# Head norms by an inverse root with one Newton step, and head sums of layer 0 in two rounded passes

## The reference

```python
def _rms_norm(x, g):
    xf = x.astype(jnp.float32)
    y = xf * lax.rsqrt(jnp.mean(xf * xf, axis=-1, keepdims=True) + EPS) * g.astype(jnp.float32)
    return y.astype(x.dtype)
...
            q = _rope(_rms_norm(q, p["q_norm_att"][j]), pos)
            k = _rope(_rms_norm(k, p["k_norm_att"][j]), pos)
...
        qx = _rms_norm(qx.reshape(n, t, N_X_HEADS, HEAD_DIM), p["q_norm_x"][i])
```

## Time and profile before

| | us |
|---|---|
| median of 3 runs (lowest, highest) | 1167.59 (1166.1, 1168.38) |
| the profiled execution | 1164.45 |
| its span, first to last instruction | 1162.7 |
| PE busy in the span | 1137.8 (98%) |
| DVE busy | 804.2 (69%) |
| ACT busy | 522.2 (45%) |
| POOL busy | 130.7 (11%) |

### The profile page before, as it was taken

How to read it: one execution, slowest core, us unless ns; L and a number is a source line. 1 busy time by engine, 2 the same in 40 slices (tenths; PEclk the granted TensorE clock), 3 DMA queues, 4 the chain that set the end, 5 groups by cost and what they waited for, 6 DMA issues and landing times.

```text
span 1162.7 us, 22189 instructions
## 1 busy us (share of the span) xinstructions
PE 1137.8 (98%) x8998; PEld 1098.3 (94%) x8998; DVE 804.2 (69%) x1201; ACT 522.2 (45%) x902; POOL 130.7 (11%) x140
## 2 busy tenths in 40 slices
PE   5999999999999999999999999999999999999998
PEld 5899646999999999999999999999999999999998
DVE  6789975798577468558658545689856846756853
ACT  7623786366136227326433232446713722732630
POOL 0038752000000000000240131200000000000000
PEclk9999999999999999999999999999999999999999
DMA  8543141223313213312622321131331332231231
GB/s 336 189 160 119 51 166 52 73 74 109 109 37 122 103 67 108 108 64 81 216 73 73 146 87 64 71 110 61 122 108 39 111 108 72 96 121 44 101 137 48
DMA packets 23146, 120.18 MB, mean 103 GB/s; under 512 B 2708, under 2 KB 6932, under 8 KB 9892
## 3 DMA queue, kind: packets, MB, share of 16 engines
q1 hardware_dynamic: 17892, 100.93, 24.7%
q0 software_dynamic: 1632, 10.54, 2.5%
q10 hardware_dynamic: 3552, 7.74, 1.9%
HBM read 111.29 MB, written 5.69 MB: 101 GB/s over the span
## 4 chain that ended last, share of the span: by engine, by line
PE 94%; DVE 2%; ACT 2%; POOL 1%; DMA 0%; issue 0%; ACTq 0%; DVEq 0%; POOLq 0%
PE zps L505 53%; PE zps L779 25%; PE ops L779 4%; PE zps L767 4%; PE tps L649 1%; PE ops L677 1%; PE tps L534 1%; POOL sm L1900 1%; DVE w_lo L929 1%; PE zps L603 1%; ACT w_hi L1410 1%; ACT act_hi L1410 1%; DVE sm L1063 0%; PE zps L610 0%; PE tps L610 0%; DMA memx<-memT 0%
## 5 line engine op out<-in xcount | busy, mean ns | idle before, releaser
L505 PE MATMUL zps<-act_hi,w_hi 128*128 128x272 f32 x1664 | 348.6, 291 | 0.9 <-DVE w_lo L929 0.9
L505 PE MATMUL zps<-act_hi,w_lo 128*128 128x272 f32 x1664 | 344.0, 288 | 0.0
L505 PE MATMUL zps<-act_lo,w_hi 128*128 128x272 f32 x1664 | 343.2, 288 | 0.0
L779 PE MATMUL zps<-xf,wf 128*128 128x272 f32 x2304 | 298.7, 289 | 0.1
L779 PEld LDWEIGHTS zps<-xf,wf 128*128 128x128 f32 x2304 | 294.1, 188 | 0.7 <-issue 0.3
L505 PEld LDWEIGHTS zps<-act_hi,w_hi 128*128 128x128 f32 x1664 | 262.2, 188 | 5.4 <-issue 2.9
L505 PEld LDWEIGHTS zps<-act_lo,w_hi 128*128 128x128 f32 x1664 | 261.5, 188 | 0.0
L505 PEld LDWEIGHTS zps<-act_hi,w_lo 128*128 128x128 f32 x1664 | 260.0, 189 | 0.0
L1410 ACT ACTIVATE w_hi<-w_stage 128x2048 fp32r<-128x2048 f32 (+1 forms) x61 | 114.7, 1883 | 151.3 <-PE zps L505 123.9
L929 DVE TENSOR_TENSOR w_lo<-w_stage,w_hi 128x2048 fp32r<-128x2048 f32 x59 | 137.6, 2333 | 43.5 <-ACT w_hi L1410 43.2
L1410 ACT ACTIVATE wf<-w_sum 128x1024 fp32r<-128x1024 f32 x64 | 67.9, 1061 | 195.4 <-DVE w_sum L947 90.4
(11 more groups left out here) (184 smaller groups left out, 1270.4 us busy)
## 6 DMA issues: line engine op xcount, KB each, us to landing
w_stage<-wst SPq DMA_DIRECT2D x92, 1024.0 KB, 4.9
kx<-xkT POOLq DMA_DIRECT2D x4, 1024.0 KB, 8.6
vx<-xv POOLq DMA_DIRECT2D x4, 1024.0 KB, 7.0
x_res<-xT ACTq DMA_DIRECT2D x2, 1088.0 KB, 7.8
tmp<-z ACTq DMA_DIRECT2D x32, 68.0 KB, 2.1
yT<-x_res ACTq DMA_DIRECT2D x7, 272.0 KB, 2.1
memx<-memT SPq DMA_DIRECT2D x2, 512.0 KB, 4.6
vb<-swav POOLq DMA_DIRECT2D x1, 1024.0 KB, 9.9
```

Source lines behind the costliest of these rows:

```text
L505: mm = pe.matmul(zps[slot][:, h, 0:n], w_[:, d, k, w:w + 128], r_[:, k, c0 + h * n:c0 + (h + 1) * n], start=(j == 0 and i == 0), stop=(j = ...
L779: mm = pe.matmul(bank, wf_hl[pw][:, fw, a, :], x_form(l, px, fx, a)[:, 0, :], start=(begin and a == 0 and j == 0), stop=(a == KC // 2 - 1 ...
```

## The change

In `root_heads` ScalarE takes Abs_reciprocal_sqrt in place of Sqrt (result y0), then squares y0 in a second instruction. VectorE, in place of the reciprocal, makes one Newton step in two SCALAR_TENSOR_TENSOR: (sum + 64 eps) y0^2, which reads `tps` again, then that minus 192, times y0; the factor -1/128 is folded into the gain (`hgain_n`, made once). The product with the gain stays. `tps` is now free for the next head sum when VectorE's first instruction is through (`n_dev`), where it was when the Sqrt was (`n_sd`).

For the ten panels of layer 0, ScalarE also rounds the squares to fp32r (`sq_hi`), VectorE forms the rest (`sq_lo`, in `square_lo`, ahead of `head_norm`), and the head sum is two fp32r products per half with a rounded block of ones (`head_r`). The two tiles lie in memory that is free in this stage. The two norms of layer 1 keep the float32 head sum.

```diff
@@ headsum
+                if n < N_QX[1]:
+                    pe.wait_ge(h_rdy, 1)
+                    pe.wait_ge(n_lo, n + 1)
+                    take(tfree)
+                    for h in range(2):
+                        c = slice(h * HALF, (h + 1) * HALF)
+                        pe.matmul(tps[:, h, 0:HALF], head_r[:, :], sq_hi[:, n % 2, c], start=True, stop=False)
+                        mm = pe.matmul(tps[:, h, 0:HALF], head_r[:, :], sq_lo[:, n % 2, c], start=False, stop=True)
+                    mm.then_inc(n_ms, 1)
+                    tfree[0] = (n_dev, n + 1)
+                    return
                 pe.wait_ge(n_sq, n + 1)
...
-                tfree[0] = (n_sd, n + 1)
+                tfree[0] = (n_dev, n + 1)
@@ head_norm
-                dve.wait_ge(n_sd, n + 1)
+                dve.wait_ge(n_inv2, n + 1)
                 taken(dve, *norm_panel(n))
-                link(dve.reciprocal(tmp[:, 3, :], tmp[:, 2, :]))
+                y0, y0_sq = tmp[:, 2, :], tmp[:, 3, :]
+                dve.scalar_tensor_tensor(out=halves(y0_sq), in0=tps[:, :, 0:HALF], scalar=HD * EPS, in1=halves(y0_sq),
+                                         op0=ALU.add, op1=ALU.mult).then_inc(n_dev, 1)
+                dve.wait_ge(n_dev, n + 1)
+                link(dve.scalar_tensor_tensor(out=y0_sq, in0=y0_sq, scalar=-3.0 * HD, in1=y0, op0=ALU.add, op1=ALU.mult))
...
+            def square_lo(n):
+                dve.wait_ge(n_hi, n + 1)
+                dve.tensor_tensor(sq_lo[:, n % 2, :], tmp[:, n % 2, :], sq_hi[:, n % 2, :].bitcast(f32), ALU.subtract).then_inc(n_lo, 1)
@@ DVE, start
+            link(dve.tensor_scalar(hgain_n[:, :], con[:, C_HG:C_HG + 4], -0.5 / HD, None, ALU.mult))
@@ DVE, loop of 12 rounds
+                if i < 10:
+                    square_lo(i)
                 if 1 <= i <= 10:
                     head_norm(i - 1)
@@ ACT, root_heads
-                root(src, dst, HD, n_ms, n + 1, n_sd, (n_out, n + 1))
+                act.wait_ge(n_ms, n + 1)
+                act.wait_ge(*sd_free[0])
+                act.activation(halves(tmp[:, 2, :]), tps[:, :, 0:HALF], ACT.Abs_reciprocal_sqrt, bias=eps, scale=1.0 / HD).then_inc(n_inv, 1)
+                act.wait_ge(n_inv, n + 1)
+                act.activation(tmp[:, 3, :], tmp[:, 2, :], ACT.Square).then_inc(n_inv2, 1)
+                sd_free[0] = (n_out, n + 1)
@@ ACT, square
                 act.activation(tmp[:, n % 2, :], norm_src(n), ACT.Square).then_inc(n_sq, 1)
+                if n < N_QX[1]:
+                    act.wait_ge(n_sq, n + 1)
+                    copy(sq_hi[:, n % 2, :], tmp[:, n % 2, :]).then_inc(n_hi, 1)
@@ ACT, start
+            copy(head_r[:, :], headones).then_inc(h_rdy, 1)
```

More of the change, by code:

```diff
@@ L92, in build_kernel @@
     sm1, _ = place("sm1", [128, 6, 260], at=at_act[1] + 12 * NT * 4)
+    sq_hi, _ = place("sq_hi", [128, 2, NT], f32r, at=at_act[1] + 12 * NT * 4)
+    sq_lo, _ = place("sq_lo", [128, 2, NT], f32r, at=at_act[1] + 14 * NT * 4)
     z1, _ = place("z1", [128, 2, NT], at=at_act[0])
@@ L122, in build_kernel @@
     con, _ = place("con", [128, C_N])
+    head_r, _ = place("head_r", [128, 128], f32r)
+    hgain_n, _ = place("hgain_n", [128, 4])
     nsink, _ = place("nsink", [128, 16])
@@ L169, in build_kernel @@
         s_full, s_sd, s_rstd = sem("s_full"), sem("s_sd"), sem("s_rstd")
-        n_sq, n_ms, n_sd, n_out = (sem("n_" + s) for s in ("sq", "ms", "sd", "out"))
+        n_sq, n_ms, n_inv, n_inv2, n_dev, n_out = (sem("n_" + s) for s in ("sq", "ms", "inv", "inv2", "dev", "out"))
+        h_rdy, n_hi, n_lo = sem("h_rdy"), sem("n_hi"), sem("n_lo")
         r_sw, r_out = [sem(f"r_sw{i}") for i in range(2)], sem("r_out")
@@ L996, in head_norm_out @@
                 src = norm_src(n)
-                dve.scalar_tensor_tensor(out=src, in0=src, scalar=hgain(norm_gain(n)), in1=tmp[:, 3, :],
+                dve.scalar_tensor_tensor(out=src, in0=src, scalar=hgain_n[:, norm_gain(n):norm_gain(n) + 1], in1=tmp[:, 3, :],
                                          op0=ALU.mult, op1=ALU.mult).then_inc(n_out, 1)
+            def square_lo(n):
+                dve.wait_ge(n_hi, n + 1)
+                dve.tensor_tensor(sq_lo[:, n % 2, :], tmp[:, n % 2, :], sq_hi[:, n % 2, :].bitcast(f32), ALU.subtract).then_inc(n_lo, 1)
             def key_sums(m):
@@ L1434, in root_heads @@
             def root_heads(n):
-                src, dst = tps[:, :, 0:HALF], halves(tmp[:, 2, :])
-                root(src, dst, HD, n_ms, n + 1, n_sd, (n_out, n + 1))
+                act.wait_ge(n_ms, n + 1)
[4 more added lines that the diff above has]
+                sd_free[0] = (n_out, n + 1)
             def square(n):
```

## The result

The changed kernel takes 1170.79 us in the median of 6 runs (1170.09 to 1171.74), the kernel before 1166.18 (6 runs, 1164.29 to 1168.38): a ratio of 1.0036, 95% interval [1.0023, 1.0049], some 4.2 us slower. 1170.9 had been forecast. The profiled execution took 1170.19 us.

The account below looks back on a forecast made before the run. PE was taken to bound the kernel, 94% of the chain. Early rounds -0.5 us, six later rounds +3.2 to +4.6, the rest 0: +3.3 taken, on the median of 1167.59 giving 1170.9 us; range 1165.0 to 1173.5.

Parts of the forecast that it names:

- Head sums: On PE in layer 0: ten head sums fall from 0.92 to 0.50 us each, 4.2 us saved if PE never waits.
- The first head sum: Rounding and rest of squares come before it, so PE starts 1.0 to 1.4 us late; 1.2 us lost.
- The table load: One more ScalarE load of 1.28 us in round 1, lying under panel 2; cost 0.
- Inverse root 0.70 and first Newton step 0.78: Durations in us assumed for ScalarE's inverse root and VectorE's first Newton step, the latter needing no port.
- rival C: Worse: first Newton step takes the port too, or release of `tps` holds the head sum; +6 to +7 us; 0.08 with D.
- The port: VectorE instructions with two SBUF inputs and GpSimd's exclude each other; demand rises from 5.97 to 7.47 us per round.
- The size of the rounds: Six rounds from 4 to 10 take 7.47 to 7.7 us in place of 6.93: +3.2 to +4.6 us.
- GpSimd's last product: The last rotary product in the stage ends 3 to 6 us later, at 127 to 131 us.
- Attention and layer 1: Attention moves as a whole, and PE does not wait for layer 1's norms; 0 us each.
- A: Rival, not slower: the port does not bind, PE gets 4.2 us less 1.2; -3.0 us, 1164.6; chance 0.20.
- B: Rival, same: one new user takes the port or both fall into GpSimd's idle time; -1 to +1.5 us, 1167.8; chance 0.20.

Follow-up runs that it names:

- a_norope: The changed kernel with GpSimd's rotary products cut to 32 of 544 columns; ratio 0.9961 to the kernel before, stage 74.15 us.
- s_only: The changed kernel with only the two rounded head-sum passes, root and reciprocal kept from the kernel before; ratio 1.0078 to the kernel before, stage 84.67 us.
- b_norope: The kernel before with GpSimd's rotary products cut to 32 of 544 columns; ratio 0.9989 to the uncut kernel before, stage 76.84 us.
- psum: The changed kernel with inverse root and second Newton result of norms 0 to 8 in PSUM; ratio 1.0008 to the kernel before, stage 79.40 us.
- twobank: The changed kernel with head sums of norms 1, 3, 5 and 7 in a second PSUM tile; ratio 1.0042 to the kernel before, stage 81.63 us.
- norest: The changed kernel without VectorE's rest of squares, the second pass rereading the rounded squares; ratio 1.0018 to the kernel before, stage 77.10 us.
- n_only: The changed kernel with only the new norm, all head sums in float32; ratio 0.9989 to the kernel before, stage 77.29 us.
- third: The changed kernel with a third buffer for the swapped halves, Newton values left in SBUF; ratio 1.0021 to the kernel before, stage 82.25 us.
- psum_third: The changed kernel with both the PSUM placement of psum and the third swap buffer of third; ratio 0.9983 to the kernel before, stage 76.64 us.
- first32: psum_third with the head sum of norm 0 in float32 again; ratio 0.9963 to the kernel before, stage 74.66 us.
- mix: psum_third with two rounded passes for odd norms only, float32 head sums for even ones; ratio 0.9971 to the kernel before, stage 74.75 us.

## Why the prediction was right

**Head sums, 4.2 saved:** right. From 58.07 to 77.66 the rounds took 6.50 to 6.58 us, where 6.51 had been worked out, and a_norope shows the 4.2 whole.

**The first head sum, 1.2 lost:** right in size; it was 1.43. PE began at 58.07, and less the run's own 0.80 that is 57.27, where 57.2 had been worked out.

**The table load, cost 0:** its size was right and its cover was not complete. ScalarE after:

```profile
59.33 0.66 ACT L1437 ACTIVATE sq_hi<-tmp 128x544 fp32r<-128x544 f32 x1
60.00 1.28 ACT L1464 ACT_TABLE_LOAD   x1
61.30 0.72 ACT L1464 ACTIVATE tmp<-tps,con 128x544 f32<-128x544 f32 x1
```

PE did not see it. But the first swap (63.94 before, 67.71 after) came later, and GpSimd began at 79.70 instead of 76.53, 2.4 us later once the run's own 0.80 is taken off. Most of that is not the load: in s_only, which has neither this load nor the square of y0, GpSimd began at 78.38 with panel 0 at 42.51, 1.8 us later than before. That leaves 0.6 us for the load and that square together. The sum had no term for GpSimd's later start. The drain of 1.38 us that the page "ScalarE: Activation LUTs" of the Trainium skill (What ACT_TABLE_LOAD costs) adds is not in this row: the load starts as the copy ends, and the inverse root starts 0.02 us after it.

**Inverse root 0.70 and first Newton step 0.78, outside the port:** 0.700 and 0.724. The first step never stretched, so rival C's premise is out.

**The port:** right, by a_norope against b_norope and by psum. The page "SBUF — State Buffer" (Terms, shared port pair) of the Trainium skill has the loser blocked for the full instruction; the rows agree (GpSimd's instruction of 79.70, 3.39 us, ends 1.22 after w_lo, its next, 1.83 us, as long after `sq_lo`), and add whose turn it is: GpSimd gets one whole instruction between two of VectorE's.

**The size of the rounds, 7.47 to 7.7 in place of 6.93:** the term that was mis-sized. The six rounds from 77.66 to 125.17 took 7.92 in the mean (6.79, 8.41, 8.50, 7.02, 8.68, 8.11). Without the clock's 1.6 us they took 7.65: the chain of turns that I had priced at 7.7 and then not taken, "nearer the lower end, since the rows carry 7.47". The rows had shown a turn on that chain too, the gain product of 1.65 at 90.22. And 7.47 was the sum of what asks for the port: no round can stay under it for long, but it is what a round takes only if the port is always in use. It was not: GpSimd, which I had said would have no idle time until the last product, stood for 6.5 us. The turn between second step and gain product cost 1.0 us in nearly every round, and in even ones w_lo and `sq_lo` back to back cost 1.2 more. So the stage was +5.7, not +3.3. The clock was in no term: it cost 1.6 us of the 5.7.

**Why the time still agreed:** that 1170.9 met 1170.79 to 0.1 us is luck. The forecast's +3.3 was too small against the 4.2 to 4.6 of the medians, and the kernel before ran 1.4 us faster beside the change than in the runs the forecast started from (1166.18 and 1167.59). The stage's 5.7 is larger than the medians' 4.2 to 4.6 for two reasons. The change wins 0.9 behind the stage. And the profile of the kernel before is one of its fastest executions, 1164.45 us with a clock of 1.0 throughout, while its median holds falls of the clock; profile against profile the change is 5.74 us slower. For the other kernels too the two differences lie up to 3 us apart; where the clock fell is known of the profiled executions alone, so this is not split further.

**GpSimd's last product:** forecast 127 to 131; it ended at 132.22 (124.60 before), 131.4 less the run's own 0.80 and so just past the range, still ahead of the scores, since panel 11 had moved too. **Attention and layer 1, 0:** right for the attention and for layer 1; between them lie the 0.9 us that came back. The release by `DVE tmp L1008` was one of the two named.

**Rivals:** A and B fall with the waits from 92.86 on. C's second half, the release of `tps`, was what PE's waits named, and twobank, whose stage is only 0.9 us shorter, shows that it was not the main cause. Of the two new users the prediction priced the rest of squares as equal to the second Newton step. It weighs more: the stage without it was 5.4 us shorter (norest), while the norm's half without it cost the stage 0.45 us against before (n_only).

## What to carry to other kernels

Before trading one long instruction for several short ones, list each one's inputs: two in SBUF beside a busy GpSimd can mean a turn of GpSimd's (1.0 to 1.2 us more here) ahead of each that follows another, so price the chain with those turns and not by its busy time. Try first whether an operand can lie in PSUM: that gave 3.3 us here with the same instructions, by the profiles some 1.3 of it in waits and 1.6 in the clock. A late engine reaches the critical one by every buffer that it frees, so a remedy for one of two such paths can show nothing until the other is mended, and a first item that has no cover may be best left in its old form. Compare the stage in the profiles and the clock of the executions before you believe a difference of 1 to 2 us between medians.

## What the runs showed of the hardware

- A VectorE instruction with one of two tensor inputs in PSUM was never held up beside GpSimd: 0.709 to 0.725 us in all ten cases of the change, seven of them with GpSimd at work, and in psum 0.728 to 0.729 and 0.780 to 0.781, where the same work in SBUF took up to 1.78.
- VectorE's instructions with two SBUF inputs back to back don't keep GpSimd out: it gets one instruction in between, and the second of VectorE's shows the wait as its own duration (0.72 to 1.88).
- Behind its waits TensorE's granted clock fell to 0.50 for some 3 us in the stage of the change, of third and of twobank, and twice in that of s_only; in the stage it stayed at 1.00 in psum, norest, psum_third, first32 and mix, but behind it it fell in norest, first32 and mix. One fall cost 1.6 to 1.7 us.
- The same stretch can be followed by a fall or not: from 156 to 160 us TensorE stood for 1.8 us in the profile of the kernel before and in that of b_norope; the clock then fell in b_norope only.
- A wait of TensorE costs 0.23 to 0.25 us more than its own length: the matmul behind it takes 0.36 instead of 0.29 us, and its round shows the rest.
